# Two attention stages of a transformer kernel rebuilt: score matmuls on half the array's rows, normalisation behind the values, the window mask added by TensorE, the rows' transposes set among the projections

## What is computed

```python
def diff_attention(q, k, v, lam, subln_g, lambda_init):      # 4 heads of 2 x 64, values 128 wide
    s = jnp.einsum('bqhcd,bkhcd->bhcqk', q_blk, k) * scale
    p = jax.nn.softmax(s, axis=-1)
    a = p[:, :, 0] - lam * p[:, :, 1]
    o = jnp.einsum('bhqk,bkhe->bqhe', a, v)
    of = o * lax.rsqrt(jnp.mean(jnp.square(o), -1) + RMS_EPS) * subln_g * (1.0 - lambda_init)

def swa_sink_attention(q, k, v, sink, mask):                 # 8 query heads, 2 of keys, 64 wide
    s = jnp.where(mask, einsum(q, k) * scale, -inf)          # |i - j| <= 128
    m = jnp.maximum(jnp.max(s, -1), sink)
    e = jnp.exp(s - m)
    p = e / (jnp.sum(e, -1) + jnp.exp(sink - m))
    o = einsum(p, v)

def hybrid_mixer(x, ...):
    h = x @ w_in                                             # 2304 columns; rotary on q and k
    return jnp.concatenate([y_diff, y_swa], -1) @ w_out
```

## Time and profile before

| | us |
|---|---|
| median of 3 runs | 1966.47 (1965.49 to 1966.47) |
| the profiled execution, its own time | 1963.66 |
| its span, first to last instruction | 1961.9 |
| PE busy, share of the span | 1823.6, 93% |
| DVE busy | 967.3, 49% |
| ACT busy | 639.9, 33% |
| POOL busy | 263.7, 13% |
| mean granted TensorE clock, as a share of 2.4 GHz | 0.964 |

### The profile page before, as it was taken

One profiled execution on the slowest core, in us unless ns is written; L12 is line 12 of the kernel. 1 busy time (PEld: TensorE's weight loads), 2 busy tenths in 40 slices (PEclk: granted clock), 3 DMA queues, 4 the chain that ended last, 5 costly groups with the idle time before them and its releaser, 6 DMA issues.

```text
span 1961.9 us, 24329 instructions
## 1 busy us (share of the span) xinstructions
PE 1823.6 (93%) x9690; PEld 1350.1 (69%) x9690; DVE 967.3 (49%) x1378; ACT 639.9 (33%) x868; POOL 263.7 (13%) x160
## 2 busy tenths in 40 slices
PE   6999988999999999899999687999998989999996
PEld 5888766788878877677887435855554767855553
DVE  3654876555555567757546895511114245511113
ACT  3534444343344334534443312210012344210010
POOL 2000540000010008020001251000000660000000
PEclk9999989999999999999999778999999999999998
DMA  6454521555455555046555101799996431799993
GB/s 270 174 191 171 214 86 44 207 182 190 178 208 183 183 187 198 1 139 221 188 181 193 43 1 64 293 421 422 422 422 249 172 113 47 298 422 421 422 422 132
DMA packets 59711, 420.44 MB, mean 214 GB/s; under 512 B 6736, under 2 KB 6736, under 8 KB 10224
## 3 DMA queue, kind: packets, MB, share of 16 engines
q1 hardware_dynamic: 55728, 404.78, 53.6%
q0 software_dynamic: 3904, 14.55, 2.2%
HBM read 418.25 MB, written 1.05 MB: 214 GB/s over the span
## 4 chain that ended last, share of the span: by engine, by line
PE 78%; DVE 14%; ACT 4%; issue 2%; POOL 1%; DMA 1%; DVEq 0%; POOLq 0%; ACTq 0%
PE h L1005 11%; PE y L562 9%; PE y L564 8%; PE y L563 8%; PE h L562 8%; PE h L564 8%; PE h L563 8%; PE turn L1031 6%; PE y L1044 3%; PE turn L929 3%; DVE w_lo L1546 2%; DVE work L1704 1%; ACT w_hi L1159 1%; DVE small L1740 1%; DVE work L1928 1%
## 5 line engine op out<-in xcount | busy, mean ns | idle before, releaser
L1546 DVE TENSOR_TENSOR w_lo<-raw,w_hi 128x2048 fp32r<-128x2048 f32 x163 | 370.6, 2290 | 153.6 <-ACT w_hi L1159 153.5
L1159 ACT ACTIVATE w_hi<-raw 128x2048 fp32r<-128x2048 f32 x193 | 364.5, 1911 | 94.6 <-DMA raw<-units 94.6
L562 PE MATMUL h<-w_hi,xt_hi 128*128 128x512 f32 x704 | 280.0, 398 | 1.1 <-DVE xt_lo L1651 0.9
L564 PE MATMUL h<-w_hi,xt_lo 128*128 128x512 f32 x704 | 275.5, 391 | 0.0
L563 PE MATMUL h<-w_lo,xt_hi 128*128 128x512 f32 x704 | 275.2, 391 | 0.0
L495 POOL TENSOR_SCALAR rstd<-moments 128x1 f32<-128x1 f32 x20 | 24.5, 1225 | 1469.1 <-DVE moments L1636 1469.1
L562 PE MATMUL y<-w_hi,xt_hi 128*128 128x512 f32 (+1 forms) x480 | 193.0, 402 | 16.7 <-ACT work L1251 4.2
L563 PE MATMUL y<-w_lo,xt_hi 128*128 128x512 f32 (+1 forms) x480 | 190.0, 396 | 0.0
L564 PE MATMUL y<-w_hi,xt_lo 128*128 128x512 f32 (+1 forms) x480 | 189.7, 395 | 0.0
L562 PEld LDWEIGHTS h<-w_hi,xt_hi 128*128 128x128 f32 x704 | 132.9, 189 | 29.3 <-DVE xt_lo L1651 2.2
L564 PEld LDWEIGHTS h<-w_hi,xt_lo 128*128 128x128 f32 x704 | 132.8, 189 | 28.4
(11 more groups left out here) (292 smaller groups left out, 2345.7 us busy)
## 6 DMA issues: line engine op xcount, KB each, us to landing
raw<-units SPq DMA_DIRECT2D x289, 1024.0 KB, 10.4
late<-units SPq DMA_DIRECT2D x96, 1024.0 KB, 11.2
ln_gb<-ln_g POOLq DMA_DIRECT2D x6, 512.0 KB, 3.8
ln_gb<-ln_b POOLq DMA_DIRECT2D x6, 512.0 KB, 5.3
x_rows<-x POOLq DMA_DIRECT2D x2, 512.0 KB, 10.8
work<-window_matrices POOLq DMA_DIRECT2D x1, 1024.0 KB, 9.8
ln_gb<-ln_mix_g POOLq DMA_DIRECT2D x2, 512.0 KB, 4.0
ln_gb<-ln_mix_b POOLq DMA_DIRECT2D x2, 512.0 KB, 5.2
```

What stands on the lines that cost most here:

```text
L562: pe.matmul(dst, left[0], right[0], start=start, stop=False)
L564: return pe.matmul(dst, left[1], right[0], start=False, stop=stop)
L1159: act.activation(hi[r][:, :], raw[r][:, :], ACT.Copy).then_inc(hi_ready, 1)
L1546: dve.tensor_tensor(lo[r][:, :], raw[r][:, :], hi[r][:, :].bitcast(F32), ALU.subtract)\
```

## The change

- **Rotary.** The products with the sine go to the PSUM bank `h_bank[t]`, no longer to SBUF, and each half t has its own buffer for the cosine.
- **Transposes.** The pairs of tile j - 1 are transposed behind projection tile j. ACT copies each query pair in one activation with the factor 1/8, into `qt1`, which has no zeros, and does so between its splits of weights.
- **Scores.** The two heads of an item are matmuls on 64 rows each, rows 0 to 63 and 64 to 127, into two different banks. Even items use the two banks `h_pair[0]`, odd ones the two of `y_pair[1]`.
- **Mask.** For a window item PE adds the masked 128 columns with two matmuls of the identity and the mask.
- **Normalisation.** A differential item becomes e0 + ratio e1, with ratio = -lambda sum0 / sum1, and a window item is transposed as the bare exponentials. The division by the sums is done once on the whole output, for both halves t (`read_diff`, and at the end the window output), now on DVE, as are the squares. Window output now uses the banks that held the differential output, so `pv(8)` and `pv(9)` wait for `diff_read`.
- **Sink.** The sink's exponentials are one activation behind item 15, no longer one for each window item.

```diff
+        y_pair, h_pair = ([ctx.enter_context(nc.psum_tensor(name, [P, TT, 512], F32)) for name in names]
+                          for names in (("y0", "y1"), ("hh",)))
+        y_bank = [[y_pair[c][:, t, :] for c in range(2)] for t in range(TT)]
+        h_bank = [h_pair[0][:, t, :] for t in range(TT)]
+        score = [h_pair[0], y_pair[1]]
...
-            pool.memset(qz1, 0.0).then_inc(zeroed, 1)
...
-                pe.wait_ge(tile_taken, seen(tile_taken, 2 * TT))
-                pe.wait_ge(row_ready, seen(row_ready, TT))
-                turn_rows(lambda m, t: qk[:, t, m * P:(m + 1) * P], 7)
+                    if j >= 1:
+                        pe.wait_ge(row_ready, seen(row_ready, TT))
+                        for r in range(*pairs[j - 1]):
+                            if r >= 2:
+                                pe.wait_ge(col_ready, seen(col_ready))
+                            for m in range(2):
+                                for t in range(TT):
+                                    at = m * T + t * P
+                                    mm = pe.transpose(turn_bank[r % 2][:, at:at + P],
+                                                      qk[:, t, (2 * r + m) * P:(2 * r + m + 1) * P], ident[:, :])
+                            mm.then_inc(row_turned, 1)
...
                     if i >= 2:
-                        pe.wait_ge(exp_ready, seen(exp_ready))
+                        pe.wait_ge(exp_ready, 16 * l + i - 1)
+                    if i == 1:
+                        pe.wait_ge(tile_taken, seen(tile_taken, TT))
+                    if i == 8:
+                        pe.wait_ge(col_ready, seen(col_ready, 2))
                     for c in range(2):
-                        mm = pe.matmul(h_bank[i % 2][:, c * T:(c + 1) * T], qz1[:, i // 2, c, t * P:(t + 1) * P],
-                                       kt1[:, k_tile, :], start=True, stop=True)
+                        rows = slice(HD * c, HD * c + HD)
+                        mm = pe.matmul(score[t][:, c, 0:T], qt1[rows, i // 2, t * P:(t + 1) * P], kt1[rows, k_tile, :],
+                                       start=True, stop=i < 8)
+                    if i >= 8:
+                        other = slice((1 - t) * P, (2 - t) * P)
+                        for c in range(2):
+                            mm = pe.matmul(score[t][:, c, other], ident[:, :], swa_mask[:, t, other], start=False, stop=True)
...
-                    pe.wait_ge(prob_ready, seen(prob_ready))
+                    if i == 0:
+                        pe.wait_ge(col_ready, seen.ahead(col_ready, 2))
+                    if i < 8:
+                        pe.wait_ge(prob_ready, 8 * l + i + 1)
+                    else:
+                        pe.wait_ge(exp_ready, 16 * l + i + 1)
...
+                        src = p1[:, i % 2] if i < 8 else e1[:, i % 2, c]
...
+                    if i in (8, 9):
+                        pe.wait_ge(diff_read, TT * l + t + 1)
...
+                split_to(8)
+                turned_rows([qt1[:, 0:2], qt1[:, 2:4]], scale=SCALE)
+                split_to(10)
+                turned_rows([kt1[:, 0:2], kt1[:, 2:4]])
+                split_to(11)
+                turned_rows([qt1[:, 4:6], qt1[:, 6:8]], scale=SCALE)
                 split_to(HYBRID_UNITS)
-                act.wait_ge(zeroed, l + 1)
-                turned_rows([qz1[:, 0:2], qz1[:, 2:4], kt1[:, 0:2], kt1[:, 2:4], qz1[:, 4:6], qz1[:, 6:8], kt1[:, 4:6]])
+                turned_rows([kt1[:, 4:6]])
...
+                    if 2 <= i < 10:
+                        act.wait_ge(prob_ready, 8 * l + i - 1)
+                    elif i >= 10:
+                        act.wait_ge(prob_turned, 16 * l + i - 1)
                     for c in range(2):
-                        src = h_bank[b][:, c * T:(c + 1) * T] if i < 8 else e1[:, b, c]
-                        ins = act.activation(e1[:, b, c], src, ACT.Exp, bias=neg[:, b, c:c + 1], scale=SCALE,
-                                             accum_out=sums[:, b, c:c + 1])
-                    if i >= 8:
-                        ins = act.activation(sink_e[:, b], sink_e[:, b], ACT.Exp)
+                        head = i // 2 if i < 8 else 2 * ((i - 8) // 2) + c
+                        neg, total = (neg_diff[:, b, c], diff_sum[:, b, c]) if i < 8 else (neg_swa[:, b], swa_sum[:, b])
+                        ins = act.activation(e1[:, b, c], score[b][:, c, 0:T], ACT.Exp, bias=neg[:, head:head + 1],
+                                             accum_out=total[:, head:head + 1])
                     ins.then_inc(exp_ready, 1)
...
+                    if i == 15:
+                        act.wait_ge(sink_ready, l + 1)
+                        act.activation(sink_e, sink_e, ACT.Exp).then_inc(sink_exp, 1)
...
-                    if i in (11, 12):
-                        if i == 11:
-                            act.wait_ge(pv_done, seen(pv_done, 8))
-                        t = i - 11
-                        for d in range(DIFF_HEADS):
-                            ins = act.activation(rot[:, t, d * P:(d + 1) * P], y_bank[t][0][:, d * P:(d + 1) * P],
-                                                 ACT.Square, accum_out=ssq[:, t, d:d + 1])
-                        ins.then_inc(squares, 1)
-                act.wait_ge(pv_done, seen(pv_done, 8))
-                for t in range(TT):
-                    act.activation(mix[:, t, 512:D], y_bank[t][1][:, :], ACT.Copy).then_inc(swa_out, 1)
...
+                by_cos = rot[:, t, 0:heads * HD].rearrange("p (h d) -> p h d", h=heads)
+                by_sin = h_bank[t][:, 0:heads * HD].rearrange("p (h d) -> p h d", h=heads)
+                if j >= 1:
+                    dve.wait_ge(row_ready, 4 * TT * l + TT * (j - 1) + t + 1)
...
-                ins.then_inc(done, 1)
-                if done is dve_link:
-                    dve.wait_ge(dve_link, seen(dve_link))
+                ins.then_inc(row_ready, 1)
...
-                    if i >= 2:
-                        dve.wait_ge(prob_ready, 16 * l + i - 1)
-                    s = h_bank[b][:, :].rearrange("p (c k) -> p c k", c=2)
...
+                    s = score[b][:, :, 0:T]
                     if i < 8:
-                        dve.tensor_scalar(neg[:, b], nmax[:, b], SCALE, None, ALU.mult).then_inc(neg_ready, 1)
+                        dve.tensor_reduce(neg_diff[:, b, :, i // 2], s, AX_X, ALU.max, negate=True).then_inc(neg_ready, 1)
...
+                def combine(i):
+
+                    b, h = i % 2, slice(i // 2, i // 2 + 1)
+                    dve.wait_ge(exp_ready, 16 * l + i + 1)
+                    link(dve.reciprocal(ratio[:, b], diff_sum[:, b, 1, h]))
+                    link(dve.tensor_scalar(ratio[:, b], ratio[:, b], diff_sum[:, b, 0, h], minus_lam[:, l:l + 1],
+                                           ALU.mult, ALU.mult))
                     if i >= 2:
                         dve.wait_ge(prob_turned, 16 * l + i - 1)
...
+                    dve.scalar_tensor_tensor(out=p1[:, b], in0=e1[:, b, 1], scalar=ratio[:, b], in1=e1[:, b, 0],
+                                             op0=ALU.mult, op1=ALU.add).then_inc(prob_ready, 1)
...
+                def read_diff(t):
+
+                    link(dve.reciprocal(diff_sum[:, t, 0], diff_sum[:, t, 0]))
+                    dve.wait_ge(pv_done, 16 * l + 7 + t)
+                    dve.tensor_tensor(heads(mix[:, t, 0:512]), heads(y_bank[t][0][:, :]),
+                                      each(diff_sum[:, t, 0], DIFF_HEADS, P), ALU.mult).then_inc(diff_read, 1)
...
+                def square(t):
+
+                    dve.wait_ge(diff_read, TT * l + t + 1)
+                    link(dve.tensor_tensor(rot[:, t], mix[:, t, 0:512], mix[:, t, 0:512], ALU.mult))
+                    dve.tensor_reduce(ssq[:, t], heads(rot[:, t]), AX_X, ALU.add).then_inc(squares, 1)
...
+                for i in range(16):
+                    maxima(i)
+                    if 1 <= i < 9:
+                        combine(i - 1)
+                    if i in (9, 10):
+                        read_diff(i - 9)
+                    if i in (11, 12):
+                        square(i - 11)
...
+                        sub_norm(i - 14)
...
+                dve.wait_ge(exp_ready, 16 * l + 16)
+                dve.wait_ge(sink_exp, l + 1)
+                link(dve.tensor_tensor(swa_sum, swa_sum, sink_e, ALU.add))
+                link(dve.reciprocal(swa_sum, swa_sum))
+                for t in range(TT):
+                    dve.wait_ge(pv_done, 16 * l + 15 + t)
+                    dve.tensor_tensor(mix[:, t, 512:D].rearrange("p (h d) -> p h d", h=SWA_Q),
+                                      y_bank[t][0][:, :].rearrange("p (h d) -> p h d", h=SWA_Q),
+                                      each(swa_sum[:, t], SWA_Q, HD), ALU.mult).then_inc(swa_out, 1)
```

120 lines of the change are left out of this document (51 added, 69 removed).

## The result

The changed kernel takes **1931.64 us** (median of 4 runs, 1928.68 to 1935.92) against 1966.47 (1965.49 to 1968.52): a ratio of 0.9823, 95% interval 0.9803 to 0.9844. Run again on another chip it took 1931.05 against 1969.26, 0.9814 (0.9794 to 0.9833). The prediction was 1934, in a range of 1924 to 1946. The profiled execution took 1932.56 us (span 1930.8), 31.1 us less than that of before; the sum had said 31.6.

A forecast was written before the change was run, and what follows sets the result against it. DVE was taken to set the pace of a mixer's stretch. 3.8 + 6.3 + 7.2 + 16.6 + 7.3 = 41.2 instead of 57.6 us, twice, plus 2.2, less 3.4 for clock, gave 31.6 and a median of 1934, range 1924 to 1946.

The forecast's parts named there:

- Transposes, 3.8 for all, gain 6.9: Before the first scores: 28 transposes cost PE 3.8 us anywhere; 24 moved among the projections gain 6.9 us per mixer.
- Rotary sum 0.7: DVE's rotary sum over 128x512, reading PSUM and SBUF, takes 0.7 us instead of 2.89.
- Scores 0.65 an item: PE's scores on paired 64-row halves: 0.44 us an item plus two tiling changes of 0.1, 0.65 in all.
- no overlap: Rival: row halves follow one another, scores 1.07 an item, 5 us lost per mixer, 1944 us; chance 8%.
- Scores 0 to 4 in 6.3, 4 to 8 in 7.2: Differential items: first four scores take 6.3 us instead of 8.57, scores 4 to 8 take 7.2 instead of 8.4.
- Window items 2.58, seven in 16.6: Scores 8 to 15: PE bounds at 2.58 us an item, seven less 1.5 make 16.6 us instead of 20.07.
- Tail 7.3: From scores 15 to the turn of `mix`: 7.3 us instead of 9.89, with a copy of 0.6 and a pass of 0.7.
- Clock, 1.7 per mixer, and 2.2 if layer 1's low spell ends: Charge of 1.7 us per mixer for low clock at attention's start; 2.2 us gained behind layer 1's turn of `mix`.
- The last step: Profiled execution 1963.66 less 31.6 is 1932.1 us; the median, 2.8 above that execution, was forecast at 1934.
- copies hold up the weights: Rival: ACT's copies delay weight splits, PE waits three times 1 to 2 us a mixer in projections, 1940 us; chance 5%.
- Low clock in a good part: Rival: low clock for 10 to 20 us of each mixer's attention costs 4.5 to 9 each, 1946 us; chance 12%.
- slower: 1.2 GHz through the attention: Rival: PE's share falls, clock stays low, attention takes 65 us instead of 46.9, 1988 us; chance 3%.

The follow-up runs named there:

- full rows: Changed kernel with each score matmul on all 128 rows, both heads' queries against both heads' keys: 1931.60 us, ratio to before 0.9815.
- the run on one half: Changed kernel with both heads' scores computed on rows 0 to 63, so halves can't work side by side: 1976.05 us, ratio to before 1.0027.
- the first profile: Profile of the unedited changed kernel in its first runs (1931.64 us); the second is from its run again on another chip (1931.05 us).

## Why the prediction was right

- **What bounds.** DVE set the pace of the window items and gave it up to PE, as said: DVE waits for PE's mask, and PE has no gap in an item.
- **Transposes, 3.8 for all, gain 6.9.** The size holds: 3.1 among the projections and 0.53 behind them. The sign given for it doesn't: the first scores stand 0.37 us behind the last tile's end and not 3 to 4, since only four of the 28 transposes are left there. The reason was incomplete. Place and sine give 2.2 per mixer, and 1.3 is the wait for the values' copies, which the prediction doesn't name. The other 3.7 are the plain copies and the clock, which it had as "ACT's copies between" and as a charge.
- **Rotary sum 0.7.** It is 0.69.
- **Scores 0.65 an item.** They take 0.63 ahead of a mask and 0.53 ahead of scores: 0.1 for a change of tiling. The Trainium skill (TensorEngine Tiling (Array Packing), section Key Properties) says that a mode switch drains the engine. The trace agrees at that small price, paid both on the way in and behind, and these drains take back most of what pairing gives against full rows. The bound for "no overlap", 1.07, is met by the run on one half (1.06). But the alternative to pairing was full rows, at 0.92, so the section overrated what that edit does. Its two changes of tiling were priced at the scores alone; the mask and the values pay 0.1 each as well.
- **Scores 0 to 4 in 6.3, 4 to 8 in 7.2.** They take 7.26 and 6.98; the start has a low clock and a wait of 1.79 for the exponentials.
- **Window items 2.58, seven in 16.6.** They take 2.55 and 16.85. The 1.5 taken off for items 8 to 10 doesn't follow from its own words, half of three times 0.66, which is 1.0; with that the sum is 17.1, and 7 x 2.55 - 16.85 = 1.0 is what the trace shows.
- **Tail 7.3.** It takes 7.43, by two misses that cancel. The terms add up to 7.2 without the copy of 0.6 and 7.8 with it. PE waits 1.12 for that copy, and the pass of 0.7 at the end isn't there: the turn of `mix` follows the values at once.
- **Clock, 1.7 per mixer, and 2.2 if layer 1's low spell ends.** In the first profile it didn't end (828.72 - 805.05 = 23.67 from turn to turn, 23.80 before), in the second it did (21.7). Against the full-clock 13.50, 7.43 and 21.7 the first profile loses 0.7 in layer 0 and 1.1, 1.9 and 2.0 in layer 1: 5.7, where the sum charged 3.4. This charge was 2.3 too small. It was made up by the stretch of layer 1 in the kernel before, which is 58.6 and not 57.6 us (timeline of PE: 835.97 - (779.72 - 2.36)), with a low clock at its start that the prediction's "happens once in each mixer now" leaves out (0.58, 0.50 and 0.64 in 780 to 792), and by projections that end 1.0 earlier in all than 3.1 us of transposes each would have them. At full clock the stages come to 3.6 + 13.5 + 16.85 + 7.43 = 41.4, forecast 41.2.
- **The last step** is off too. For the profiled execution the sum said 1932.1, and it took 1932.56. The 2.8 us added for the median make 1934.9 and not 1934, and they aren't there: the changed kernel's median lies 0.9 below its profiled run. That the sum comes within 0.5 us is luck in part, since the misses above, of up to 2.3 us, cancel.
- **Rivals.** *No overlap* is excluded, *copies hold up the weights* too: PE has no such wait. *Low clock in a good part* didn't come, and *slower: 1.2 GHz through the attention* didn't either, but the run on one row half shows what it would be: 63.30 of 64 us busy, at 0.52, 70 us for one attention where the rival reckoned 65, and the gain gone. Its reason, a fallen share of busy time, is neither shown nor excluded. In 266 to 268 us, ahead of the fall, PE was busy for 1.30 of 2 us in that run, and while the clock was low the share was high.
